# The order of VectorE's work in the attention head loop: logits and normalisations of a head pair side by side, then token shifts, evictions and selection rounds

## The chip, the cores and the metric

The kernel runs on one core of one Trainium2 chip. Its time is the device time of one launch in microseconds (us); shown are the median, the lowest and the highest of three runs, and one more execution was recorded by the hardware profiler. The engines are called by the profile's names: PE (TensorE, with PEld for its weight loads), DVE (VectorE), ACT (ScalarE), POOL (GpSimd) and SP (SyncE).

## The reference, cut to what matters

A step of a two-layer encoder over 512 prompt tokens and 64 sample tokens, `D_MODEL` 1024. Each layer projects the normalised input with one wide matrix (`w_in`); its columns go to three branches (RWKV-7 time mixing, sparse attention, retention) and to gates. The change lies in the sparse attention and in what runs beside it, the first steps of the RWKV branch:

```python
# sparse attention: an indexer scores keys, the best topk of them are kept for each query
score = einsum(relu(qi . ki), wi) * INDEX_SCALE          # masked to admissible keys
_, idx = lax.top_k(score, topk)                          # 128 of up to 512, 144 for the sample
logits = einsum(q, k_sel) * SA_HEAD_DIM ** -0.5
p = softmax(logits)
o = einsum(p, v_sel)                                     # 8 heads, 2 key/value heads
...
# RWKV: token shift of the projected columns P, 14 tiles of 128 columns
X = P + (prev - P) * rwkv_mu                             # prev: the row before, per token
```

## The kernel before, in words

All activations are kept transposed, 128 channels on the partitions and tokens (576 = 512 + 64) along the free axis. Projections run in float32 split into a high and a low part, so one slice of a dense tile (128 output columns, 128 of the 1024 inputs) is six matmuls of 288 columns, and a tile has `KT = 8` slices. Weights come by SP's queue, POOL splits them, and PE multiplies. Every engine executes a program of its own, in the order in which it is written out by hand, and waits on semaphores where it needs another.

The stage of the change is the **head loop** of each layer's sparse attention. There are 40 runs: run = 8 * b + h, with four blocks `b` of 128 queries (128, 256, 384 and 512 keys) and h = 0 to 7 heads, and then block 4, the 64 sample queries. Runs 0 to 31 are taken in 16 pairs (run, run + 1); even runs use half 0 and odd runs half 1 of the PSUM and SBUF buffers. A head goes through these steps:

- `scores` (PE, L559): query times keys into `mix[half]`. It first waits until the logits of run - 2 have left that buffer.
- `logits` (DVE, L1981 and L1984): scales, adds the mask of the selected keys, takes the row maximum and its negative.
- `exps` (ACT): the exponential and its row sum (an ACTIVATE and a READ_ACCUMULATOR).
- `normalised` (DVE, L2084 and L2086): reciprocal of the sum, then the multiplication of the probabilities.
- `turn_head` (PE, L984) transposes the probabilities, `turned_head` (ACT) copies them, `values` (PE) multiplies them by v, `out_head` (ACT) copies the result out. `turn_head(run)` waits for `normalised(run)` and for `out_head(run - 2)`.

Three other things are done beside the heads. PE **fills**: after `turn_head` of a pair it multiplies the next slices of the RWKV and gate projections, 10 slices a pair in blocks 0 to 2 and 8 in block 3 (`FILL_STEP`). A finished tile is evicted from PSUM by DVE: `shift_raws` (L2054 to L2061) multiplies it by the row norms into the two-buffered `pt`, or, for the tiles from 14 on, `gate_scaled` (L2040) does so into a gate buffer; both free the PSUM buffer. ACT's `filled` then multiplies `pt` by `mu` into the single buffer `d_t` (or, for a gate, starts the store to memory with `gate_away`), and DVE's `token_shift` (L2069) adds the other half and frees `d_t` with `shift_dve`. And DVE does the **selection rounds** of the next blocks (`rounds_beside`: `topk`, each round a MAX8 L1949 and a MATCH_REPLACE8 L1951, each behind a drain L1675); `STEP_ROUNDS` says which rounds belong to which run.

DVE's order in an iteration of the pair loop is: the rounds of run, `normalised` of both heads, `shift_raws` of the tiles that ended in the fill of the pair before (`arrived`), the rounds of run + 1, `token_shift` of the same tiles, `logits` of the next pair. ACT's order is `out_head` of the pair before, `turned_head` of this pair, `filled`, `exps` of the next pair. Counted from the two lists (`fill_range`, `done`), `arrived` holds one tile in most iterations, two at runs 8, 16 and 24 (tiles 4 and 5, 9 and 10, 14 and 15). At run 2, the rotary step of tile 15 (`rope`, L1715 to L1721) stands first.

Of the kernel before, what the change touches and what calls it, by code (L numbers as in the profile page):

```python
# [38 lines left out]
KT = D // P  # L39
# [20 lines left out]
N_RET, N_SA, N_RW, N_GATE = 16, 9, 14, 24  # L60
# [87 lines left out]
def fill_range(b, h):  # L148

    first = KT + 8 * sum(FILL_STEP[:b]) + h * FILL_STEP[b]  # L150
    return first, first + FILL_STEP[b]


def mid_range(step):
# [13 lines left out]
def done(first, end):  # L168

    return range(first // KT, end // KT)  # L170
# [55 lines left out]
def build(nc, dr, outs):  # L226
    with ExitStack() as ctx:
# [907 lines left out]
        def _(act):  # L1135
# [206 lines left out]
            with act.Fori(0, DEPTH) as l:  # L1342
# [65 lines left out]
                def exps(b, h):  # L1408
                    n, keys = (P, (b + 1) * P) if b < 4 else (C, T)
                    half, run = h % 2, b * 8 + h  # L1410
                    act.wait_ge(at_logits, l * 40 + (run + 1))
                    if run >= 2:

                        act.wait_ge(at_turned, l * 40 + (run - 1))
                    op(prob[0:n, half, 0:keys], logit[0:n, half, 0:keys], ACT.Exp,
                       bias=stat[0:n, half, 1:2], accum_out=stat[0:n, half, 2:3]).then_inc(at_exp, 1)

                piece = 0
                for t in range(3, N_SA):
# [14 lines left out]
                    if t >= 5:  # L1434
                        b = t - 4
# [17 lines left out]
                def filled(tiles):  # L1453

                    for f in tiles:
                        if f >= N_RW:
                            gate_away(l, f - N_RW, gate_dsa)
                            continue
                        act.wait_ge(shift_raw, l * N_RW + (f + 1))
                        if f >= 1:  # L1460
                            act.wait_ge(shift_dve, l * N_RW + f)
                        op(d_t, pt[:, f % 2, 0:TX], ACT.Copy, scale=pr("mu", f)).then_inc(shift_mu, 1)
# [57 lines left out]
                waiting = [0]  # L1520
                ended = [[], []]
                for run in range(0, 32, 2):
                    b, h = run // 8, run % 8
                    if run:
                        out_head(run - 2)
                        out_head(run - 1)
                    turned_head(run)
                    turned_head(run + 1)
                    filled(waiting)
                    waiting = list(done(fill_range(b, h)[0], fill_range(b, h + 1)[1]))  # L1530
                    if run < 30:
                        for r in (run + 2, run + 3):
                            exps(r // 8, r % 8)
                out_head(30)
                for run in range(31, 40):
                    b, h = run // 8, run % 8
# [133 lines left out]
        def _(dve):  # L1670
# [216 lines left out]
            with dve.Fori(0, DEPTH) as l:  # L1887
# [203 lines left out]
                    for rounds in STEP_ROUNDS.get(run, ()):  # L2091
                        topk(*rounds)

                arrived = [0]
                logits(0, 1)
                for run in range(0, 32, 2):
                    b, h = run // 8, run % 8
                    if run == 2:
                        rope(l, 15, s_raw, s_tcos, s_trot, s_cos, s_sin, ysa[:, 3, :])
                        settle()  # L2100

                    rounds_beside(run)
                    normalised(run)
                    normalised(run + 1)
                    shift_raws(arrived)
                    rounds_beside(run + 1)
                    token_shift(arrived)
                    arrived = list(done(fill_range(b, h)[0], fill_range(b, h + 1)[1]))
                    if run < 30:
                        for r in (run + 2, run + 3):  # L2110
                            logits(r // 8, r % 8)
                assert all(t >= N_RW for t in arrived)
                shift_raws(arrived)
                logits(4, 0)

                ended = []
# [269 lines left out]
```

## Time and profile before

| | |
|---|---|
| time, median of 3 runs | 2569.2 us |
| lowest and highest | 2565.81 and 2570.72 us |
| time of the profiled execution | 2568.46 us |
| its span, first to last instruction | 2566.7 us |
| busy PE, PEld, DVE, ACT, POOL | 2481.8, 2351.5, 1221.2, 588.8, 1344.2 us |
| mean granted TensorE clock | 0.982 |
| head loop of layer 0, pairs 0 to 30 | about 240 to 412 us of the span |
| the same of layer 1 | about 1510 to 1682 us |

The page gives the busy time of each engine over the whole span; the other views give groups of instructions, waits, the chain of work that ended last, and the instructions in order of time. A clock of 1.00 is 2.4 GHz, 0.50 is 1.2 GHz. Times of instructions are us from the start of the span.

### The profile page before, as it was taken

Reading aid. Unit: us, or ns where it says so; the run is one execution under the profiler, and the core shown is the slowest. Engines: PE = TensorE matmul, PEld = TensorE weight load, DVE = VectorE, ACT = ScalarE, POOL = GpSimd, SP = SyncE. Lnnn points to the kernel's source line nnn. Section 1 sums busy time; section 2 is a strip of 40 time slices with the busy share of each in tenths; the row PEclk is TensorE's granted clock in tenths of the full one; section 3 lists DMA queues with packets and bytes.
Section 4 is the critical chain, followed back from the end, with each engine's and each line's share of the span. In section 5 each row is a group of like instructions: output and inputs, shape, how many; then the busy total and the mean of one; then the engine's idle time right before and its main releaser. Section 6 shows DMA issues by size and latency. Waiting matters only on the chain.

```text
span 2566.7 us, 62432 instructions
## 1 busy us (share of the span) xinstructions
PE 2481.8 (97%) x24614; PEld 2351.5 (92%) x24614; DVE 1221.2 (48%) x2248; ACT 588.8 (23%) x1155; POOL 1344.2 (52%) x1780
## 2 busy tenths in 40 slices
PE   8998999999989999999999989999999899999998
PEld 7997888899979999999999978888999799999998
DVE  5357886544465322121443578856544653121224
ACT  4122233322232211011230223233221422010112
POOL 7634443512137766666775445434222477666665
PEclk9999999999999999999999999999999999999999
DMA  5212112311144222222242221223111442222221
GB/s 207 92 38 90 58 59 97 116 40 41 42 166 152 82 89 83 82 82 82 82 151 71 68 77 58 72 80 115 41 36 61 173 138 83 83 83 82 82 82 70
DMA packets 67690, 223.78 MB, mean 87 GB/s; under 512 B 8736, under 2 KB 9632, under 8 KB 66432
## 3 DMA queue, kind: packets, MB, share of 16 engines
q1 hardware_dynamic: 44496, 159.08, 18.5%
q10 hardware_dynamic: 22960, 61.34, 6.9%
q8 instruction: 177, 2.90, 0.5%
q14 instruction: 57, 0.47, 0.1%
HBM read 190.25 MB, written 29.03 MB: 85 GB/s over the span
## 4 chain that ended last, share of the span: by engine, by line
PE 85%; DVE 7%; DVEq 4%; issue 2%; ACT 1%; DMA 1%; ACTq 1%; POOL 0%; SPq 0%
PE dense L559 70%; PE mix L559 13%; DVEq L1675 3%; DVE region_b L1949 1%; DVE region_b L2069 1%; DVE region_b L1981 1%; PE mix L984 1%; POOL w_lo L546 0%; DVE region_b L2086 0%; DMA region_b<-region_b 0%; ACT in_hi L1137 0%; DVE x L1951 0%; DVE x L1967 0%; ACT region_b L1137 0%; DVE region_b L2055 0%
## 5 line engine op out<-in xcount | busy, mean ns | idle before, releaser
L542 POOL TENSOR_SCALAR w_hi<-w_raw 128x512 fp32r<-128x512 f32 x592 | 381.7, 663 | 1177.0 <-PE dense L559 928.9
L546 POOL TENSOR_TENSOR w_lo<-w_raw,w_hi 128x256 fp32r<-128x256 f32 x1184 | 962.5, 844 | 24.7
L559 PE MATMUL dense<-in_hi,w_hi 128*128 128x288 f32 x2432 | 680.0, 294 | 16.2 <-DVE in_lo L2181 15.3
L559 PE MATMUL dense<-act_hi,w_hi 128*128 128x288 f32 x2272 | 677.1, 309 | 17.5 <-POOL w_lo L546 12.6
L559 PE MATMUL dense<-in_lo,w_hi 128*128 128x288 f32 x2432 | 679.1, 295 | 0.0
L559 PE MATMUL dense<-act_lo,w_hi 128*128 128x288 f32 x2272 | 652.4, 298 | 0.0
L559 PE MATMUL dense<-act_hi,w_lo 128*128 128x288 f32 x2272 | 538.7, 298 | 0.0
L559 PE MATMUL dense<-in_hi,w_lo 128*128 128x288 f32 x2432 | 522.9, 297 | 0.0
L559 PEld LDWEIGHTS dense<-in_hi,w_hi 128*128 128x128 f32 x2432 | 459.1, 189 | 18.5 <-DVE in_lo L2181 16.8
L559 PEld LDWEIGHTS dense<-act_hi,w_hi 128*128 128x128 f32 x2272 | 436.1, 192 | 35.5 <-DVE act_lo L1693 11.1
L559 PEld LDWEIGHTS dense<-in_lo,w_hi 128*128 128x128 f32 x2432 | 459.4, 189 | 0.0
L559 PEld LDWEIGHTS dense<-act_lo,w_hi 128*128 128x128 f32 x2272 | 436.6, 192 | 0.0
L559 PEld LDWEIGHTS dense<-in_hi,w_lo 128*128 128x128 f32 x2432 | 390.8, 189 | 0.0
L559 PEld LDWEIGHTS dense<-act_hi,w_lo 128*128 128x128 f32 x2272 | 387.0, 191 | 0.0
L2248 DVE SCALAR_TENSOR_TENSOR y_mix<-dense,n_root 128x576 f32<-128x576 f32 x64 | 48.5, 758 | 296.6 <-PE dense L559 282.9
L1137 ACT ACTIVATE y_mix<-y_mix 128x576 f32<-128x576 f32 x64 | 44.0, 687 | 604.0 <-DVEq L2251 604.0
L1137 ACT ACTIVATE region_b<-region_b 128x576 f32<-128x576 f32 (+7 forms) x166 | 106.3, 642 | 312.8 <-DVE region_b L1984 115.5
L1137 ACT ACTIVATE region_b<-mix 128x256 f32<-128x256 f32 (+5 forms) x194 | 77.9, 419 | 344.7 <-PE mix L559 242.1
L2263 DVE TENSOR_TENSOR x<-x,dense 128x576 f32<-128x576 f32 x48 | 36.2, 755 | 252.6 <-PE dense L559 252.6
L559 PE MATMUL mix<-region_b 64*64 64x64 f32 (+5 forms) x2008 | 121.2, 240 | 2.5 <-ACT y_mix L1137 2.5
L559 PEld LDWEIGHTS mix<-region_b 64*64 64x64 f32 (+3 forms) x2008 | 101.5, 142 | 20.6 <-issue 19.3
L1137 ACT ACTIVATE region_b<-dense 128x256 f32<-128x256 f32 (+4 forms) x134 | 64.5, 494 | 191.0 <-PE dense L559 137.6
(201 smaller groups left out, 2513.8 us busy)
## 6 DMA issues: line engine op xcount, KB each, us to landing
w_raw<-in_stream SPq DMA_DIRECT2D x296, 512.0 KB, 3.3
region_b<-gate_scratch ACTq DMA_DIRECT2D x48, 288.0 KB, 2.9
gate_scratch<-region_b ACTq DMA_DIRECT2D x36, 288.0 KB, 2.2
x_scratch<-x ACTq DMA_DIRECT2D x2, 2304.0 KB, 13.2
y_scratch<-y_mix ACTq DMA_DIRECT2D x2, 2304.0 KB, 7.5
x<-x_scratch ACTq DMA_DIRECT2D x2, 2304.0 KB, 10.1
y_mix<-y_scratch ACTq DMA_DIRECT2D x2, 2304.0 KB, 9.0
gate_scratch<-region_a ACTq DMA_DIRECT2D x12, 288.0 KB, 2.4
```

Source lines behind the costliest of these rows:

```text
L542: hi = nc.gpsimd.tensor_scalar(w_hi[:, v, c], w_raw[:, s, c], 1.0, 1.0, ALU.mult, ALU.mult)
L546: lo = nc.gpsimd.tensor_tensor(w_lo[:, v, c], w_raw[:, s, c], w_hi[:, v, c].bitcast(F32), ALU.subtract)
L559: return nc.tensor.matmul(out, lhsT, rhs, start=start, stop=stop, skip_group_check=True)
L984: mm = nc.tensor.transpose(out[half][0:w, kb * n:(kb + 1) * n], prob[0:n, half, kb * P:kb * P + w], ident[0:n, 0:n])
L1137: return nc.scalar.activation(out, in_, func, **kw)
L1675: v.drain()
L1949: v.max(out=top8[0:n], in_=sc)
L1981: v.tensor_tensor_reduce(logit[0:n, half, 0:keys], mix[half][0:n, 0:keys], sa_bias[b][0:n, 0:keys], SA_SCALE, -3.0e38, ALU.add, ALU.max, s ...
L2069: v.scalar_tensor_tensor(shifted[t], pt[:, t % 2, 1:TX + 1], mu_own[:, t:t + 1], d_t, ALU.mult, ALU.add).then_inc(shift_dve, 1)
L2248: v.scalar_tensor_tensor(halves(relu_m[:, m % 2, :]), out_of(dense[m % 2]), 0.0, halves(n_rs), ALU.max, ALU.mult).then_inc(dense_free[m % ...
L2263: v.tensor_tensor(halves(x[:, m, :]), halves(x[:, m, :]), out_of(dense[m % 2]), ALU.add).then_inc(dense_free[m % 2], 1)
```

## The change

DVE's iteration becomes: `normalised` of both heads of the pair (right behind the `logits` that ended the iteration before), the rotary step at run 2, `token_shift` of the tiles that were evicted before, `shift_raws` of the late tiles of the pair before, the rounds of run and of run + 1 in one piece, `shift_raws` of the early tiles of this same pair, `logits` of the next pair. A new function `pair_done` names the tiles that end in a pair's fill and counts those that end in its first four slices as early. ACT does `filled` behind `exps` of the next pair, not ahead of it, for the late tiles of the pair before and the early ones of this pair. By the two lists, the early tiles are 3, 4, 8, 9, 13 and 14 (evicted at runs 4, 6, 12, 14, 20 and 22), all others are late, and `token_shift` has two tiles at runs 6, 14 and 22 (tiles 2 and 3, 7 and 8, 12 and 13). PE's program is not changed.

```diff
@@ -149,6 +149,14 @@
     first = KT + 8 * sum(FILL_STEP[:b]) + h * FILL_STEP[b]
     return first, first + FILL_STEP[b]
+def pair_done(run):
+    first, end = fill_range(run // 8, run % 8)[0], fill_range(run // 8, run % 8 + 1)[1]
+    tiles = list(done(first, end))
+    return tiles, sum(1 for t in tiles if (t + 1) * KT - first <= 4 and run < 30)
 def mid_range(step):
@@ -1526,11 +1534,12 @@
                         out_head(run - 1)
                     turned_head(run)
                     turned_head(run + 1)
-                    filled(waiting)
-                    waiting = list(done(fill_range(b, h)[0], fill_range(b, h + 1)[1]))
                     if run < 30:
                         for r in (run + 2, run + 3):
                             exps(r // 8, r % 8)
+                    tiles, early = pair_done(run)
+                    filled(waiting + tiles[:early])
+                    waiting = tiles[early:]
                 out_head(30)
                 for run in range(31, 40):
                     b, h = run // 8, run % 8
@@ -2091,26 +2100,28 @@
                     for rounds in STEP_ROUNDS.get(run, ()):
                         topk(*rounds)
-                arrived = [0]
+                shifting, late = [], [0]
                 logits(0, 1)
                 for run in range(0, 32, 2):
-                    b, h = run // 8, run % 8
+                    normalised(run)
+                    normalised(run + 1)
                     if run == 2:
                         rope(l, 15, s_raw, s_tcos, s_trot, s_cos, s_sin, ysa[:, 3, :])
                         settle()
+                    token_shift(shifting)
+                    shift_raws(late)
                     rounds_beside(run)
-                    normalised(run)
-                    normalised(run + 1)
-                    shift_raws(arrived)
                     rounds_beside(run + 1)
-                    token_shift(arrived)
-                    arrived = list(done(fill_range(b, h)[0], fill_range(b, h + 1)[1]))
+                    tiles, early = pair_done(run)
+                    shift_raws(tiles[:early])
+                    shifting, late = late + tiles[:early], tiles[early:]
                     if run < 30:
                         for r in (run + 2, run + 3):
                             logits(r // 8, r % 8)
-                assert all(t >= N_RW for t in arrived)
-                shift_raws(arrived)
+                assert all(t >= N_RW for t in shifting + late)
+                shift_raws(late)
                 logits(4, 0)
                 ended = []
```

## Rows read from the trace of the kernel before

**Rows 1.** Page: busy us (share of the span) and instructions, by engine

```profile
PE 2481.8 (97%) x24614; PEld 2351.5 (92%) x24614; DVE 1221.2 (48%) x2248; ACT 588.8 (23%) x1155; POOL 1344.2 (52%) x1780
```

**Rows 2.** Busy time by stage of layer 0: span, engines, clock, DMA

```profile
235.00:412.00 177.00, 166.05 (x1187) 150.69 (x1186) 148.93 (x424) 50.92 (x139) 78.05 (x111) 0.94 0.19 64
```

**Rows 3.** Waits of 225 to 415 us: engine, line, releaser, total, times, longest

```profile
PE mix L984 <- DVE region_b L2086: 9.5, 5, 3.0
...
DVE region_b L2069 <- ACT region_b L1137: 2.1, 3, 0.9
```

**Rows 4.** Timeline of PE, layer 0: transposes; start, us, [idle before]

```profile
255.78 0.88 PE L984 MATMUL mix<-cst,region_b 128*128 128x128 f32 x2 [2.88 <-DVE region_b L2086]
...
347.51 1.51 PE L984 MATMUL mix<-cst,region_b 128*128 128x128 f32 x6 [3.00 <-DVE region_b L2086]
...
382.88 1.09 PE L984 MATMUL mix<-cst,region_b 128*128 128x128 f32 x8
383.73 0.38 PE L559 MATMUL dense<-act_hi,w_hi 128*128 128x288 f32 x1
```

**Rows 5.** Timeline of PE, layer 1, the transpose of run 18

```profile
1617.28 1.51 PE L984 MATMUL mix<-cst,region_b 128*128 128x128 f32 x6 [3.00 <-DVE region_b L2086]
```

**Rows 6.** PE by stretch around run 18: busy, granted clock, DMA

```profile
347.50:352.50 5.00, 4.99 (x22) 0.50 0.03 11
```

**Rows 7.** Timeline of DVE at the loop's start

```profile
239.78 0.15 DVE L1984 TENSOR_SCALAR region_b<-region_b 128x1 f32<-128x1 f32 x1
...
242.24 0.16 DVE L2084 RECIPROCAL region_b<-region_b 128x1 f32<-128x1 f32 x1
...
242.91 0.15 DVE L2084 RECIPROCAL region_b<-region_b 128x1 f32<-128x1 f32 x1
```

**Rows 8.** Timeline of ACT at the loop's start

```profile
241.07 0.59 ACTq L1451 DMA_DIRECT2D out_ik_new<-region_b  x1
...
242.09 0.19 ACT L1137 ACTIVATION_READ_ACCUMULATOR region_b<-region_b 128x1 f32 x1
```

**Rows 9.** Timeline of DVE, normalisation, two-tile shift, logits' end

```profile
284.98 0.16 DVE L2084 RECIPROCAL region_b<-region_b 128x1 f32<-128x1 f32 x1
...
285.49 0.15 DVE L2084 RECIPROCAL region_b<-region_b 128x1 f32<-128x1 f32 x1
...
286.12 0.13 DVE L2054 COPY region_b<-par 128x1 f32<-128x1 f32 x1
...
291.73 0.82 DVE L2069 SCALAR_TENSOR_TENSOR region_b<-region_b,mu_own 128x577 f32<-128x577 f32 x1
293.46 0.82 DVE L2069 SCALAR_TENSOR_TENSOR region_b<-region_b,mu_own 128x577 f32<-128x577 f32 x1 [0.91 <-ACT region_b L1137]
...
365.77 0.16 DVE L1984 TENSOR_SCALAR region_b<-region_b 128x1 f32<-128x1 f32 x1
```

**Rows 10.** Timeline of ACT, mu product and exponentials

```profile
292.64 0.78 ACT L1137 ACTIVATE region_b<-region_b,par 128x577 f32<-128x577 f32 x1 [4.78 <-DVE region_b L2069]
...
296.54 0.19 ACT L1137 ACTIVATION_READ_ACCUMULATOR region_b<-region_b 128x1 f32 x1
296.63 0.55 ACT L1137 ACTIVATE y_mix<-mix 64x128 f32<-64x128 f32 x2
...
366.48 0.19 ACT L1137 ACTIVATION_READ_ACCUMULATOR region_b<-region_b 128x1 f32 x1
```

**Rows 11.** Timeline of DVE, rounds and normalisations of run 24, gates

```profile
378.71 0.74 DVE L1949 MAX8 region_b<-x 64x8 f32<-64x576 f32 x1
...
380.42 0.16 DVE L2084 RECIPROCAL region_b<-region_b 128x1 f32<-128x1 f32 x1
...
381.30 0.61 DVE L2086 TENSOR_SCALAR region_b<-region_b 128x512 f32<-128x512 f32 x1
381.83 1.40 DVE L2040 TENSOR_TENSOR region_a<-dense,n_root 128x576 f32<-128x576 f32 x2
```

**Rows 12.** Timeline of DVE behind the pair loop

```profile
421.72 0.76 DVE L2040 TENSOR_TENSOR region_a<-dense,n_root 128x576 f32<-128x576 f32 x1 [6.61 <-PE dense L559]
```

## Prediction

> **What bounds the kernel now.** The page comes first: PE is busy for 2481.8 of 2566.7 us, DVE for 48% of it [rows 1]. Over the span PE sets the time, and whatever DVE does is worth only what PE waits for it. The second view is therefore the busy time of the stage alone. In the head loop of layer 0 PE is busy for 166.05 of 177 us and DVE for 148.93, and the granted clock is 0.94 [rows 2]; the reader is to see that here DVE is no longer at half load. Third, the waits of that stretch: PE's transposes wait for the normalisation (L2086) five times, 9.5 us in total and 3.0 at the longest, while DVE waits for ACT's mu product three times, 2.1 us in all [rows 3]. The view names no wait of DVE for PE between the first pair and the end of the selection rounds. DVE's other free time lies between its own instructions, in drains. Fourth, the timeline of PE: the long waits are at run 2 (2.88 us) and run 18 (3.00 us) [rows 4], and layer 1 has 3.00 us at run 18 as well [rows 5]. Right behind the wait of run 18 PE runs for 5.00 us at a granted 0.50, the 1.2 GHz level [rows 6], so such a wait costs up to 2.5 us more.
>
> The point that I take from this: from the first pair on **DVE's own chain is the slow one** and PE keeps up with it. Behind run 18 PE no longer waits, but it is just in time: at run 24 the second normalisation ends at 381.30 + 0.61 = 381.91 and PE's transposes begin at 382.88, a slack of 0.97 us [rows 4, 11]. So DVE may be late by about one us there before PE is late, and a gain is limited likewise. Behind the loop there is room: DVE sits idle for 6.61 us before the last gate eviction [rows 12].
>
> **The change part by part.** No operation is added or removed; DVE's sum of work stays. What changes is what DVE has done by each normalisation, since this releases PE, and where DVE waits for ACT. I follow DVE to the normalisation of run 24, the first pair behind the last iterations with much work (20 and 22), where the slack is 0.97. All terms are per layer.
>
> *The rounds go behind the normalisation.* At run 24 one round of 576 keys no longer stands in front: from 378.71 to 380.42 [rows 11], **-1.71**. That is the gain of the change. At run 2 the rotary step goes behind too, so the wait of 2.88 should vanish; but DVE does that work afterwards and the next pairs get it.
>
> *A gate eviction goes ahead.* Tile 14 is early at run 22 and so comes before the normalisation of run 24. Two took 1.40 us [rows 11]: **+0.70**. The other tiles up to 13 are evicted and shifted before that point in either order.
>
> *The start.* Before, the rounds of run 0 hid ACT's lateness. The logits of run 1 end at 239.78 + 0.15 = 239.93, the second reciprocal came 0.67 us behind the first [rows 7], and so DVE would get to it at about 240.6 if the first starts at once. But ACT issues transfers (the last begins at 241.07, 0.59 us) and the sum of exponentials of run 1 is read only at 242.09 + 0.19 = 242.28 [rows 8]. With no rounds in between DVE sits idle for 242.3 - 240.6 = **+1.7**. PE gains 0.6 there, which does not help the chain.
>
> *The normalisations wait for the exponentials.* At run 22 the second logits end at 365.77 + 0.16 = 365.93 and the second sum is read at 366.48 + 0.19 = 366.67 [rows 9, 10], 0.74 us later. In an unbroken normalisation pair the second reciprocal comes 284.98 to 285.49 = 0.51 behind the first [rows 9], so some 0.58 behind the logits. The wait is up to 0.16; with fewer keys the exponential is shorter. For 12 pairs (runs 2 to 24) the bounds are 0 and 1.9; I take 0.12 each, since the row of run 22 is a long one: **+1.4**.
>
> *The token shift waits for the mu product.* `filled` now stands behind the exponentials. ACT starts an instruction 0.09 behind the start of such a read (296.54, 296.63), so the product, 0.78 us long [rows 10], ends about 0.74 - 0.10 + 0.78 = 1.42 behind the logits. DVE gets to the shift after the pair of normalisations, 286.12 - 284.98 = 1.14 [rows 9], and is there 1.2 to 1.37 behind the logits. Before, a set of rounds hid the product. Ten pairs (4 to 22), bounds 0 and 2.1, I take 0.13 each: **+1.3**.
>
> *Two tiles at once.* The second product needs `d_t` free and so waits for the first shift: 291.73, product at 292.64, second shift at 293.46 after 0.91 us idle [rows 9, 10]. This exists before and after; now it comes at three iterations (6, 14, 22), and all waits of this kind took 2.1 before [rows 3]: 3 x 0.91 - 2.1 = **+0.6**.
>
> Sum: -1.71 + 0.70 + 1.7 + 1.4 + 1.3 + 0.6 = **+4.0** on DVE's chain at run 24; by the low bounds +1.3, by the high ones +5.3. PE's share is 4.0 - 0.97 = 3.0. The reader should also follow ACT: in the two-tile iterations its second `filled` waits for a shift of the next iteration, and `out_head` and with it PE's transposes stand behind it, some 2 us longer than the normalisation alone would keep them. At run 22 this is covered by the wait at run 24 that follows; without that cover it is up to 2 us more. The gate stores start later on ACT's queue, but two iterations pass before their buffer is wanted again: nothing.
>
> Last, the clock. DVE's heavy iterations (late and early evictions at 20, two shifts at 22) now follow each other, so I expect PE to wait for about 3 us at run 24, as at run 18 before. Whether the clock falls there and costs 2.5 us [rows 6] is open; bounds 0 and 2.5 in each layer. PE has only the slack of its last pairs to win it back. I take it in one of two layers. Total: 2 x 3.0 + 2.5 = **+8.5 us** on the profiled execution's 2568.46 us (span 2566.7 and 1.8 around it): **2577.0 us**. That execution lies 0.7 under the median of the runs shown, 2569.2. About 0.2%, 5.1 us, is what a measurement of this kernel can tell from no change.
>
> **The rivals.**
>
> *A: the waits of DVE for ACT are hidden.* If the normalisation and shift terms are near 0, DVE is late by 1.3 and PE by 0.3: 2569.1 us; with half of those terms, PE is 1.7 late without a fall of the clock: 2571.9. For it: the exponential of the first head is done before the second logits are, and each wait that I charge is under 0.2 us. Against it: the start alone costs what the rounds give. This is no measurable change.
>
> *B: faster, because PE is what sets the loop.* Then its waits go away: 9.5 us per layer [rows 3]. The mechanism: each pair's probabilities are ready one set of rounds earlier, and a wait of 3.0 would fall to 1.3 by the 1.71 us of a single round, and further where two rounds stood in front. It decides if DVE has time to spare, so that the work put behind the normalisations is done while PE fills. With all waits gone 2568.5 - 19 = 2549.5; with a third, 2562. The Trainium skill, Perfetto Trace Analysis, Identifying the Most-Contended Engine, would take the engine with the highest occupancy as the bottleneck, and for TensorE weight loads, not matmuls; in this stage that is 150.69 us of weight loads against 148.93 of DVE, so by that rule PE stays in front and the time is B's. Against B: DVE's rest is no waiting for PE, and from run 24 on the slack is under one us.
>
> *C: slower by more.* All waits at their high bounds, 5.3 - 0.97 = 4.3, the clock falls in both layers: 2 x (4.3 + 2.5) = 13.6, 2582; with `out_head` behind the product 2 us more in each layer, 2586. For it: every one of these chains goes through ACT's single queue.
>
> **How the numbers follow.** Forecast (2574.5 without a fall of the clock to 2579.5 with two): 0.48. A: 0.27. B: 0.11. C: 0.14. Faster is B, 0.11; the same is A, 0.27; slower is the forecast and C, 0.62. For 8 in 10 the range leaves out most of B and the end of C: 2565 to 2586.
>
> **What would show it.** Right, if the profile of the changed kernel has DVE idle for 1.5 to 2 us before a reciprocal at the start of each loop with ACT as the releaser; small waits of reciprocals and shifts for ACT in nearly every pair; three waits of 0.9 at shifts; PE without a wait at run 2 and with long ones at runs 8, 16 and 24; and the transposes of run 30 some 3 to 5 us later from the loop's start than before. Wrong, if PE has no wait behind run 10, or if those last transposes come no later: then DVE's chain was not the limit or its waits were covered.

## The result, and the profile of the changed kernel

The changed kernel takes 2581.73 us (median of six runs, 2577.95 to 2584.06) beside 2568.97 (six runs, 2565.57 to 2572.3): a ratio of 1.005, 95% interval 1.0038 to 1.0061. It is slower. The profiled execution takes 2581.09 us with a span of 2579.3, against 2568.46 and 2566.7: +12.6, where +8.5 was forecast.

The head of the page answers to [rows 1]:

```profile
PE 2489.6 (97%) x24614; PEld 2355.3 (91%) x24614; DVE 1225.4 (48%) x2248; ACT 585.8 (23%) x1155; POOL 1342.4 (52%) x1780
```

The counts of instructions are the same, so no work was added; DVE's sum has grown by 4.2 us all the same, to which the last parts come back. Next, the waits of 225 to 425 us in layer 0 (engine, line, releaser: total, times, longest), which answer to [rows 3]. PE's transposes are now L992, its other products L567, the reciprocals L2093, the multiplications L2095, the token shift L2078, the first instruction of an eviction L2063, the end of the logits L1993.

```profile
PE mix L992 <- issue: 5.5, 3, 2.3
...
PE mix L567 <- DVE region_b L1993: 4.4, 6, 1.8
...
DVE region_b L2093 <- ACT region_b L1145: 3.6, 9, 1.9
...
DVE region_b L2063 <- issue: 2.9, 13, 0.2
PE mix L992 <- ACT y_mix L1145: 2.8, 4, 0.9
DVE region_b L2078 <- ACT region_b L1145: 2.7, 3, 0.9
...
PE mix L992 <- DVE region_b L2095: 1.1, 2, 0.7
```

PE's waits for normalisations have gone from 9.5 us to 1.1. In their place stand three waits put down to "issue" (that is, to nothing the view can name), waits of the score products for logits, and waits for ACT's copies. DVE's own idle time is of several kinds, shown one by one below.

The first stands at the start of the loop; DVE's timeline there (start, duration, instruction, idle before it and its releaser) answers to [rows 7]:

```profile
236.71 0.15 DVE L2093 RECIPROCAL region_b<-region_b 128x1 f32<-128x1 f32 x1
236.94 0.29 DVE L2095 TENSOR_SCALAR region_b<-region_b 128x128 f32<-128x128 f32 x1
239.18 0.16 DVE L2093 RECIPROCAL region_b<-region_b 128x1 f32<-128x1 f32 x1 [1.94 <-ACT region_b L1145]
```

The second is one of the three two-tile iterations, on DVE, ACT and PE in turn:

```profile
272.67 0.82 DVE L2078 SCALAR_TENSOR_TENSOR region_b<-region_b,mu_own 128x577 f32<-128x577 f32 x1
274.39 0.82 DVE L2078 SCALAR_TENSOR_TENSOR region_b<-region_b,mu_own 128x577 f32<-128x577 f32 x1 [0.90 <-ACT region_b L1145]
```

```profile
271.88 0.76 ACT L1145 ACTIVATE region_b<-region_b,par 128x577 f32<-128x577 f32 x1
273.58 0.78 ACT L1145 ACTIVATE region_b<-region_b,par 128x577 f32<-128x577 f32 x1 [0.95 <-DVE region_b L2078]
274.27 0.55 ACT L1145 ACTIVATE y_mix<-mix 64x128 f32<-64x128 f32 x2
```

```profile
274.62 0.30 PE L992 MATMUL mix<-cst,region_b 128*128 128x128 f32 x1 [2.16 <-issue]
...
323.55 0.45 PE L992 MATMUL mix<-cst,region_b 128*128 128x128 f32 x1 [2.26 <-issue]
...
373.74 0.30 PE L992 MATMUL mix<-cst,region_b 128*128 128x128 f32 x1 [1.10 <-issue]
```

Read across: the second mu product on ACT sits 0.95 us for DVE's first shift; `out_head`'s copies to `y_mix` stand behind it in ACT's queue, and PE's transposes go as soon as the first copy is done. So the "issue" waits of PE at runs 6, 14 and 22 are the hold behind the second `filled`; I call them the holds. Behind the first two the clock falls in this layer, behind the third it does not; PE's stretches that begin at these transposes (length; PE busy; granted clock; DMA) answer to [rows 6]:

```profile
274.60:279.60 5.00, 4.98 (x25) 0.66 0.01 2
323.50:328.50 5.00, 4.95 (x21) 0.50 0.01 3
373.70:378.70 5.00, 4.96 (x38) 1.00 0.00 0
```

Third, one iteration with a single shift:

```profile
284.82 0.16 DVE L2093 RECIPROCAL region_b<-region_b 128x1 f32<-128x1 f32 x1 [0.17 <-ACT region_b L1145]
285.06 0.57 DVE L2095 TENSOR_SCALAR region_b<-region_b 128x256 f32<-128x256 f32 x1
285.56 1.16 DVE L2078 SCALAR_TENSOR_TENSOR region_b<-region_b,mu_own 128x577 f32<-128x577 f32 x1
286.95 0.15 DVE L2063 COPY region_b<-par 128x1 f32<-128x1 f32 x1 [0.24 <-issue]
```

A small wait for the exponentials (0.17), no wait for the mu product, and a gap of 0.24 before the eviction, where an eviction directly behind a normalisation began 0.08 before that one's end [rows 11].

At run 24 the fill starts without a wait, DVE's two reciprocals, then PE; this answers to [rows 4, 11]:

```profile
384.52 0.15 DVE L2093 RECIPROCAL region_b<-region_b 128x1 f32<-128x1 f32 x1
...
385.49 0.16 DVE L2093 RECIPROCAL region_b<-region_b 128x1 f32<-128x1 f32 x1 [0.24 <-ACT region_b L1145]
```

```profile
385.78 1.22 PE L992 MATMUL mix<-cst,region_b 128*128 128x128 f32 x8
386.75 0.38 PE L567 MATMUL dense<-act_hi,w_hi 128*128 128x288 f32 x1
```

These times cannot be set against those of before directly, since the loops begin at different places. I count from a `memset` of DVE at the loop's head (239.05 and 1509.12 us before, 235.91 and 1515.61 after), which I call the origin. Three marks are used from here on: the first reciprocal of run 24 (384.52 - 235.91 = 148.61 after, 380.42 - 239.05 = 141.37 before), the loop's length (up to the logits of the tail head that follows the pair loop), and PE's dense work at run 24 (386.75 - 235.91 = 150.84 against 383.73 - 239.05 = 144.68). In the changed kernel DVE reaches run 24 later by 7.24 us (6.69 in layer 1), PE fills later by 6.16, and the loop is longer by 6.34 us in layer 0 and 6.60 in layer 1. The two sum to 12.9, against 12.6 in the span. The three stretches outside the loops (ahead of the first, between them, behind the second) differ by -3.1, +3.3 and -0.5 us, which sum to -0.3: on balance the whole loss lies in the two head loops.

### The profile page after: what moved, and what is told of

Same layout as the page of the kernel before. It is cut to its first block, busy times and chain, and to the rows that moved or that the text cites. A ratio compares the mean times of both kernels' runs of the same rounds, so it can differ in the third digit from the quotient of the medians.

```text
span 2579.3 us, 62432 instructions
## 1 busy us (share of the span) xinstructions
PE 2489.6 (97%) x24614; PEld 2355.3 (91%) x24614; DVE 1225.4 (48%) x2248; ACT 585.8 (23%) x1155; POOL 1342.4 (52%) x1780
## 4 chain that ended last, share of the span: by engine, by line
PE 83%; DVE 7%; DVEq 4%; issue 3%; ACT 2%; ACTq 1%; DMA 1%; POOL 0%; SPq 0%
PE dense L567 69%; PE mix L567 13%; DVEq L1684 3%; DVE region_b L1958 2%; ACT region_b L1145 1%; DVE region_b L1990 1%; DVE region_b L2078 1%; PE mix L992 0%; POOL w_lo L554 0%; ACT in_hi L1145 0%; DMA region_b<-region_b 0%; DVE region_b L2065 0%; DVE x L1960 0%; ACTq L1218 0%; ACTq L1219 0%
## 5 line engine op out<-in xcount | busy, mean ns | idle before, releaser
L550 POOL TENSOR_SCALAR w_hi<-w_raw 128x512 fp32r<-128x512 f32 x592 | 374.9, 651 | 1191.5 <-PE dense L567 951.5
L567 PE MATMUL dense<-in_hi,w_hi 128*128 128x288 f32 x2432 | 680.1, 294 | 15.2 <-DVE in_lo L2192 14.6
L567 PE MATMUL dense<-act_hi,w_hi 128*128 128x288 f32 x2272 | 678.5, 309 | 15.7 <-POOL w_lo L554 12.1
L567 PE MATMUL dense<-in_lo,w_hi 128*128 128x288 f32 x2432 | 679.1, 295 | 0.0
L567 PE MATMUL dense<-act_lo,w_hi 128*128 128x288 f32 x2272 | 653.5, 299 | 0.0
L567 PE MATMUL dense<-act_hi,w_lo 128*128 128x288 f32 x2272 | 539.3, 299 | 0.0
L567 PE MATMUL dense<-in_hi,w_lo 128*128 128x288 f32 x2432 | 523.0, 296 | 0.0
L567 PEld LDWEIGHTS dense<-in_hi,w_hi 128*128 128x128 f32 x2432 | 459.4, 189 | 18.0 <-DVE in_lo L2192 16.1
L567 PEld LDWEIGHTS dense<-act_hi,w_hi 128*128 128x128 f32 x2272 | 436.5, 192 | 32.8 <-DVE act_lo L1702 11.0
L567 PEld LDWEIGHTS dense<-in_lo,w_hi 128*128 128x128 f32 x2432 | 459.7, 189 | 0.0
L567 PEld LDWEIGHTS dense<-act_lo,w_hi 128*128 128x128 f32 x2272 | 437.0, 192 | 0.0
L567 PEld LDWEIGHTS dense<-in_hi,w_lo 128*128 128x128 f32 x2432 | 391.1, 189 | 0.0
L567 PEld LDWEIGHTS dense<-act_hi,w_lo 128*128 128x128 f32 x2272 | 387.5, 192 | 0.0
L567 PE MATMUL mix<-region_b 64*64 64x64 f32 (+5 forms) x2008 | 121.0, 240 | 2.5 <-ACT y_mix L1145 2.5
L567 PEld LDWEIGHTS mix<-region_b 64*64 64x64 f32 (+3 forms) x2008 | 101.3, 142 | 20.7 <-issue 19.4
```

The lines of the kernel that those rows point to most:

```text
L550: hi = nc.gpsimd.tensor_scalar(w_hi[:, v, c], w_raw[:, s, c], 1.0, 1.0, ALU.mult, ALU.mult)
L567: return nc.tensor.matmul(out, lhsT, rhs, start=start, stop=stop, skip_group_check=True)
```

## The experiments

All times are medians; "before" is the kernel before, run beside it. The ratio and its interval are taken over the single runs, so the ratio is not quite the quotient of the two medians. "Run 24" and "loop" are the marks above, for layers 0 / 1, from one profiled execution of each kernel. The two layers run the same loop and their marks differ by up to 1.6 us, so a difference well under that is not to be trusted.

| kernel | us | before, us | ratio (95%) | run 24 | loop |
|---|---|---|---|---|---|
| before | 2568.97 | | | 141.37 / 141.62 | 183.83 / 183.25 |
| changed | 2581.73 | 2568.97 | 1.005 (1.0038-1.0061) | 148.61 / 148.31 | 190.17 / 189.85 |
| e1_start | 2578.26 | 2568.35 | 1.0041 (1.0026-1.0055) | 146.01 / 146.29 | 189.33 / 188.19 |
| e2_act | 2578.28 | 2568.35 | 1.0041 (1.0026-1.0055) | 147.12 / 146.63 | 189.07 / 188.60 |
| e3_evict_first | 2579.49 | 2568.35 | 1.0034 (1.0019-1.0048) | 145.73 / 144.92 | 187.74 / 186.70 |
| e4_norm_only | 2583.84 | 2568.35 | 1.0068 (1.0051-1.0085) | 147.51 / 146.86 | 192.45 / 191.89 |
| e5_two_mu | 2577.77 | 2566.43 | 1.0036 (1.0019-1.0052) | 146.40 / 145.93 | 188.41 / 187.65 |
| e6_all_three | 2560.19 | 2566.43 | 0.998 (0.996-0.9999) | 142.08 / 141.52 | 183.80 / 183.60 |
| e7_before_two_mu | 2560.59 | 2566.43 | 0.9971 (0.9954-0.9988) | 139.25 / 139.15 | 182.50 / 180.93 |
| e8_norm_evict | 2569.73 | 2566.43 | 1.0006 (0.999-1.0022) | 142.49 / 143.87 | 185.43 / 186.92 |
| e9_before_fewer | 2563.41 | 2569.54 | 0.9973 (0.9959-0.9986) | 136.62 / 137.09 | 179.50 / 180.10 |
| e9_after_fewer | 2566.93 | 2569.54 | 0.9991 (0.9982-1.0001) | 141.70 / 141.00 | 183.26 / 182.53 |

The theory: DVE's chain sets the head loop, and the change adds idle time and slower instructions to that chain. The rivals: ACT's hold of `out_head` is what costs, through PE's waits and clock; or PE sets the loop and DVE's lateness is covered.

**e1_start.** One cost is taken away: run 0's rounds go back ahead of the first normalisation.

```
                 for run in range(0, 32, 2):
+                    if run == 0:
+                        rounds_beside(run)
                     normalised(run)
                     normalised(run + 1)
...
-                    rounds_beside(run)
+                    if run:
+                        rounds_beside(run)
                     rounds_beside(run + 1)
```

> The changed kernel, but the rounds of run 0 stand ahead of the first normalisations again. Theory 1 (VectorE's own chain up to the normalisation of run 24 sets the loop, and its idle wait of 1.94 us for ScalarE's first exponential is part of what was added): the chain is 1.8 us shorter per layer and TensorE follows in full, 3.5 us below the changed kernel, about 9 us above the kernel before. Theory 2 (ScalarE's queue, with the copies of the results behind the mu products, sets TensorE): the wait at the start is not what counts, no more than 1 us of change. Theory 3 (the clock): no change, 12 to 13 us above.

DVE's chain at run 24 shortens by 2.60 / 2.02 us, but the loop only by 0.84 / 1.66. PE's transposes at run 22 show why:

```profile
374.70 1.51 PE L992 MATMUL mix<-cst,region_b 128*128 128x128 f32 x6 [2.15 <-issue]
```

With DVE earlier, the hold at run 22 is 2.15 us where it was 1.10, and behind it the granted clock over 5 us is 0.50 where it was 1.00, so in layer 0 part of the gain goes into the next limit. In layer 1 the hold was 2.15 already and the clock behind it is 1.00 where it was 0.66; there the loop follows by most of the gain. The start wait is real and costs what was forecast or a little more; the hold, with the clock behind it, is a second limit close behind.

**e2_act.** ACT's order: the waiting tile's product goes ahead of the exponentials, only the early tile's stays behind them.

```
                     turned_head(run + 1)
+                    filled(waiting)
                     if run < 30:
...
-                    filled(waiting + tiles[:early])
+                    filled(tiles[:early])
```

> The changed kernel, but ScalarE makes the mu product of the late tiles ahead of the exponentials of the next pair, as before the change; only the early tiles' products stay behind them. Theory 1: the shift of a single tile does not wait for ScalarE in the changed kernel's trace, so VectorE's chain stays, within 1 us of the changed kernel. Theory 2: the copies of the results come 0.8 us sooner in most pairs and TensorE's transposes with them, 4 to 8 us below the changed kernel.

Run 24 is earlier by 1.49 / 1.68 and the loop shorter by 1.10 / 1.25, more than the first theory had and far from the second. The three holds stay (2.00, 2.09 and 2.06 us at runs 6, 14 and 22), so this order of ACT does not make them.

The expectation had one thing wrong: single shifts do wait for the product, by less than the 0.15 us that the views name. In the changed kernel seven of the ten shifts behind a normalisation in layer 0, and eight in layer 1, start 0.03 to 0.04 us behind the end of ACT's product. Run 4, ACT and DVE in the changed kernel:

```profile
260.69 0.76 ACT L1145 ACTIVATE region_b<-region_b,par 128x577 f32<-128x577 f32 x1
```

```profile
261.06 0.29 DVE L2095 TENSOR_SCALAR region_b<-region_b 128x128 f32<-128x128 f32 x1
261.48 0.82 DVE L2078 SCALAR_TENSOR_TENSOR region_b<-region_b,mu_own 128x577 f32<-128x577 f32 x1
```

The product ends at 261.45, 0.10 behind the normalisation's end. With the product done early the same shift starts 0.09 ahead of that end:

```profile
259.42 0.29 DVE L2096 TENSOR_SCALAR region_b<-region_b 128x128 f32<-128x128 f32 x1
259.62 0.81 DVE L2079 SCALAR_TENSOR_TENSOR region_b<-region_b,mu_own 128x577 f32<-128x577 f32 x1
```

Over the ten shifts this run takes 0.80 / 1.07 us of such idle time away.

**e3_evict_first.** On DVE the late eviction goes ahead of the shift, so that it follows a normalisation again.

```
-                    token_shift(shifting)
                     shift_raws(late)
+                    token_shift(shifting)
```

> The changed kernel, but the evictions of the late tiles come ahead of the token shifts, right behind the normalisations. Theory 1: of what VectorE's chain has gained in length some 0.24 us per iteration is the gap ahead of an eviction that follows a shift and its drain; behind a normalisation there was none before. Nine evictions of that kind: 2.1 us less per layer, 4 us below the changed kernel. If the gap moves to the shift instead, or the evictions now wait for TensorE: 0 to 1 us. Theory 2: no change.

By the marks this is the largest single effect: 2.88 / 3.39 at run 24 and 2.43 / 3.15 in the loop. The timed runs do not rank e1, e2, e3 and e5 (ratios 1.0034 to 1.0041), and the profiled execution of e3 was no shorter than that of the changed kernel, as the stretches outside its loops took 6.3 us more. The waits of DVE name where it comes from:

```profile
DVE region_b L2063 <- issue: 1.0, 5, 0.2
```

The gap ahead of an eviction is gone in eight of its 13 places, 1.9 us of named idle time. The rest is less exactly placed: evictions and shifts also ran shorter, 0.82 and 0.34 us in layer 0, and normalisations 0.72 longer (sums of all their rows).

**e4_norm_only.** From the other side: the kernel before, with only its normalisations moved ahead of the rotary step and of the rounds of `run`; evictions and shifts stay behind them.

```
                     b, h = run // 8, run % 8
+                    normalised(run)
+                    normalised(run + 1)
                     if run == 2:
...
                     rounds_beside(run)
-                    normalised(run)
-                    normalised(run + 1)
                     shift_raws(arrived)
```

> The kernel before, but the normalisations of a pair stand ahead of the rounds of run; evictions, shifts, early and late tiles and ScalarE's order are those before the change. Theory 1: VectorE's chain at run 24 has +1.8 from the start, +2 from the exponentials and -1.7 from the round that goes behind, 2.1 us; less 1 us of slack that is 1.1 us per layer: 2 us above the kernel before, 10 below the changed kernel, so most of the loss is from the other half of the change. Theory 2: ScalarE's queue is that of before, so none of the loss is left: at the kernel before or up to 5 us below it, as the probabilities come earlier.

It is the slowest of all, 192.45 / 191.89, and some 15 us above the kernel before, where one theory had 2 above and the other none. Of its waits of PE over the whole program the longest in sum is this:

```profile
PE dense L559 <- DVEq L2060: 20.1, 14, 3.4
```

Before, this wait (PE's dense work for an accumulator in PSUM that DVE has yet to evict) was 1.4 us in four. In DVE's list the evictions stand behind the same work as before; but the fill now starts a set of rounds sooner, and so asks for its accumulators sooner than they are free. DVE's chain is also late by 6.14 / 5.24 at run 24, with waits for the exponentials (3.9 us in ten in layer 0, six of them up to run 24) and gaps ahead of the evictions (2.2 in ten); this run does not part the two. What follows: an earlier normalisation alone moves PE's wait from the transposes to the accumulators, so moving the evictions too was a necessary part of this change.

**e5_two_mu.** The changed kernel with a second mu buffer, in space that is free during the loop, so that the second product need not wait for the first shift.

```
+        d_two = [d_t, region_b[:, cw.at - 2 * T:cw.at - 2 * T + TX]]
...
-                        if f >= 1:
-                            act.wait_ge(shift_dve, l * N_RW + f)
-                        op(d_t, pt[:, f % 2, 0:TX], ACT.Copy, scale=pr("mu", f)).then_inc(shift_mu, 1)
+                        if f >= 2:
+                            act.wait_ge(shift_dve, l * N_RW + f - 1)
+                        op(d_two[f % 2], pt[:, f % 2, 0:TX], ACT.Copy, scale=pr("mu", f)).then_inc(shift_mu, 1)
...
-                        v.scalar_tensor_tensor(shifted[t], pt[:, t % 2, 1:TX + 1], mu_own[:, t:t + 1], d_t, ALU.mult,
+                        v.scalar_tensor_tensor(shifted[t], pt[:, t % 2, 1:TX + 1], mu_own[:, t:t + 1], d_two[t % 2], ALU.mult,
...
```

> The changed kernel with a second buffer for the mu product (tiles in turn), so that ScalarE's second product no longer waits for VectorE's first shift, and the copies of the results behind it are not held. Theory 1 (VectorE's chain): three waits of 0.90 us go, the chain at run 24 is 2.7 us shorter per layer. Theory 2 (the hold in ScalarE's queue at runs 6, 14 and 22, seen as waits of 2.2 us of TensorE's transposes): the transposes of these runs come 2 us sooner as well, and the clock does not fall behind them. Both together: 5 to 8 us below the changed kernel, 5 to 8 above the kernel before; if neither is on the path: no change.

Run 24 is earlier by 2.21 / 2.38, the loop shorter by 1.76 / 2.20; the time is 4 us under the changed kernel, less than the 5 to 8 expected. DVE's wait for the product (2.7 us in three) is gone from the waits, and PE's holds are now these:

```profile
PE mix L993 <- issue: 3.4, 3, 1.2
```

The holds fell by 2.1 us, so the single buffer makes that part of them; what keeps PE for the other 1.1 to 1.2 us each was not looked into. DVE's chain fell by 2.2, so this run alone does not tell the chain from ACT's hold as the cause. e3 does: it leaves the "issue" waits nearly as they were (4.9 us in three, before it 5.5), with the waits for ACT's copies even longer (4.6 us, before it 2.8), and still shortens the loop by more than e5.

**e6_all_three.** e1, e3 and e5 together, in the changed kernel.

> The changed kernel with all three: the rounds of run 0 ahead, the late evictions ahead of the shifts, two buffers for the mu product. Theory 1: the chain at run 24 falls by 2.4 + 3.1 (as measured singly) + 2.7 = 8.2 us from 148.5, to 140 us behind the loop's start, 1 us ahead of the kernel before, and nothing holds TensorE at runs 6, 14 and 22: 0 to 3 us below the kernel before. If TensorE's own work or another hold sets the loop by now, only half of that comes: 4 to 7 us above the kernel before.

The loop is 183.80 / 183.60 us, that of the kernel before (183.83 / 183.25). The single effects on run 24 sum to 7.69 / 7.79 and together give 6.53 / 6.79. So taking the three away wins back as much as was lost. Not all of that was the loss, though: the second buffer also takes away waits that the old order has (e7). Against e7, with that buffer on both sides, the new order's loops are still longer by 1.30 / 2.67 us and its run 24 later by 2.83 / 2.37; in the timed runs the two cannot be told apart (2560.19 and 2560.59). With the three costs gone the new order is worth nothing against the old one.

**e7_before_two_mu.** The second mu buffer of e5, in the kernel before.

> The kernel before with only the second buffer for the mu product. Theory 1: its two waits of 0.91 us per layer and the small one go from a chain that bounds the loop; TensorE has 1 us of slack there, so it gains what its own work lets it: 1 to 2 us per layer, 2 to 4 us below the kernel before. If TensorE's work behind run 18 sets the end: the wait of 3.0 us at run 18 falls by 1.8, 3 to 4 us in all; if neither: no change.

The simplest version that beats both: 2560.59 us, 0.1 to 0.5% under the kernel before, with one buffer more and the old order. Run 24 is earlier by 2.12 / 2.47 and the loops are shorter by 1.33 / 2.32. The two shifts that were 291.73 and 293.46, with 0.91 us between them [rows 9], now run on:

```profile
291.56 1.74 DVE L2070 SCALAR_TENSOR_TENSOR region_b<-region_b,mu_own 128x577 f32<-128x577 f32 x2
293.65 0.43 DVE L1982 CUSTOM_DVE_ANT_0 region_b<-mix,x 128x256 f32<-128x256 f32 x1 [0.35 <-issue]
```

Taking some 2 us of waiting out of DVE's chain shortens the loop by two thirds to nearly all of it: in the kernel before, too, DVE's chain carries the loop.

**e8_norm_evict.** The kernel before with two mu buffers and, from run 2 on, normalisations, then evictions, ahead of the rounds; the shifts stay behind the rounds, where their products are covered.

```
+                    if run == 0:
+                        rounds_beside(run)
+                    normalised(run)
+                    normalised(run + 1)
                     if run == 2:
...
-                    rounds_beside(run)
-                    normalised(run)
-                    normalised(run + 1)
                     shift_raws(arrived)
+                    if run:
+                        rounds_beside(run)
                     rounds_beside(run + 1)
                     token_shift(arrived)
```

> The kernel before with the normalisations ahead of the rounds (but not at run 0), the evictions of the pair before right behind them, then all rounds, then the shifts; ScalarE's queue as before the change, two buffers for the mu product; no early tiles. Theory 1: at run 24 -1.7 for the round that goes behind, -2.1 for the waits for mu, +1.5 to 2 for the waits for the exponentials: 2 us less chain than before; 2 to 6 us below the kernel before. Theory 2 (TensorE's work and holds): the waits at runs 2, 10 and 18 go, 5 to 10 us below.

No measurable change against the kernel before, where both theories had it faster, and slower than e7 by 9 us, with loops longer by 2.93 / 5.99. Of PE's waits over the whole program this one is new:

```profile
PE mix L560 <- DVE region_b L1985: 12.1, 12, 2.2
```

At the transposes PE waits for normalisations for 3.9 us, where e7 has 23.3. What it no longer waits for there it waits for at the scores, because the logits come later by the rounds that were moved. Normalising early with its costs removed brings nothing.

**e9_before_fewer and e9_after_fewer.** Both kernels without the selection rounds of runs 2 to 5, 9.6 us of DVE's time in each layer.

```
                     for rounds in STEP_ROUNDS.get(run, ()):
-                        topk(*rounds)
+                        if not 2 <= run <= 5:
+                            topk(*rounds)
```

> The kernel before without the selection rounds of runs 2 to 5 (eight rounds, 9.6 us of VectorE in each layer; the selection is then not the reference's). Theory 1 (VectorE's chain sets the loop's length): the normalisation of run 24 comes 9.6 us sooner and the loop is shorter by as much as TensorE's own work allows; the waits at runs 10 and 18 (5.8 us) and the falls of the clock behind them (up to 5 us) go: 6 to 9 us per layer, 12 to 18 us below the kernel before. If TensorE sets it: at most 2 us below.

> The changed kernel without the same rounds. Theory 1: the chain falls by 9.6 us from 148.5 us to 139 us at run 24 and the loop with it, 8 to 9.6 us per layer: 4 to 7 us below the kernel before, still some 10 us above the kernel before without the same rounds. Theory 2 (holds in ScalarE's queue): the holds at runs 6, 14 and 22 stay, with three falls of the clock: 0 to 4 us above the kernel before. If TensorE's own work sets it: no change, 12 us above.

The changed kernel's loop gives 6.91 / 7.32 of the 9.6 us back, that of the kernel before only 4.33 / 3.15. In the latter DVE's shifts then wait for ACT's product for 6.3 us in layer 0, where it was 2.1 [rows 3], and one of these waits is new and long:

```profile
DVE region_b L2069 <- ACT region_b L1137: 6.3, 4, 4.1
```

It stands at run 4, where rounds were taken out that had covered it: the product comes behind `out_head`'s copy, and that copy waits 4.08 us for PE's product with v. In the changed kernel DVE meets a limit too, 2.69 us before the early eviction of run 4:

```profile
264.23 0.15 DVE L2063 COPY region_b<-par 128x1 f32<-128x1 f32 x1 [2.69 <-PE dense L567]
```

So at the place where the rounds went, DVE's chain is longer than that of PE and ACT by only some 3 to 4 us a layer in the kernel before, and by some 7 in the changed one; rounds of other runs were not tried. I had expected 6 to 9 in the kernel before and 8 to 9.6 in the changed one, which came out some 2.6 us under the kernel before, not clear of noise, and not 4 to 7: the two chains lie closer together than my theory had it.

## Why the prediction was right, and where its sum was wrong

The sign, the place and the range are right: slower, through DVE's chain in the two head loops, 2581.7 within 2565 to 2586. The forecast of +8.5 us was 4.1 short, and its sum holds errors of opposite sign.

**What bounds the kernel.** Right. e6, e7 and e9 show that the loop's length follows DVE's chain. The slack of PE at run 24 is as read in layer 0: the chain is late by 7.24 and PE's dense work by 6.16, so 1.08 was absorbed, forecast 0.97. The forecast took the same for layer 1, and there it does not hold: before the change the second normalisation ended at 1652.22 and PE's transposes began at 1652.34, a slack of 0.12, and 0.22 was absorbed (6.69 on the chain, 6.47 on PE's dense work).

**DVE's chain at run 24.** This is the step that failed in size: +4.0 forecast, +7.24 / +6.69 measured. Layer 0, term by term:

- Rounds behind: one round less stands in front, as forecast (DVE's 576-key scans up to that point are 6 where they were 7), -1.57 by its instructions' durations against -1.71 from start to start.
- Gate ahead: forecast +0.70, measured 0.76 by its duration.
- Start: forecast +1.7, measured 1.94 of idle time (1.87 more than between two other such instructions), and e1 gives 2.60 / 2.02 back.
- Normalisations: forecast +1.4. Eight waits for the exponentials are named, 3.6 - 1.94 = 1.7 us, six of them up to run 24. By all rows the idle time inside the pairs grows by 4.42, of which 1.87 is the start, so 2.5; but the normalisations themselves run 1.66 us shorter in sum, so the net is 0.9.
- Shifts of single tiles: forecast +1.3, measured 1.0. No such wait is named, but most of the ten shifts behind normalisations start as the product ends. On average they start 0.01 us behind the normalisation's end (0.03 in layer 1), where those that find the product done start 0.08 ahead of it; e2 gives 0.80 / 1.07 back.
- Two tiles: forecast +0.6, measured 3 x 0.90 - 1.82 = 0.88.

These give some 3.8, near the 4.0 forecast, so the terms of the sum were about right in total. The other 3.4 us stood in no term, and that is where the sum failed. They come from all rows of DVE's timeline between the origin and run 24, durations and the idle time between them summed for each kind. Instructions that stand in front of run 24 in both kernels run longer, by 2.9 us in sum: selection rounds 1.1, the rotary step 0.9, shifts 0.6, evictions 0.4, logits -0.1. Idle time within the groups (other than normalisations and pairs of shifts) grows by 1.1. Between the groups it grows by 0.4, and without the waits of the shifts it shrinks by 0.6. Of the gaps between groups, eight of 0.23 between shift and eviction, five of 0.22 between rounds and an early eviction and six of 0.33 between rounds and logits come in; twelve of 0.35 between shift and logits go out, with smaller ones. In layer 1 the rotary step and the rounds run longer by about as much, the evictions by 0.7, the shifts not. My error was to price a moved instruction at its old duration and its old distance to its neighbour.

**The clock.** Forecast a fall behind a long wait at run 24 worth 2.5 us in one of two layers. PE had no wait there and its fill ran at full clock. The clock fell at other places: over 5 us it is 0.66 behind run 6 and 0.50 behind run 14, where the kernel before has 0.50 behind each of its long waits at runs 2, 10 and 18; in layer 1 it is 0.66 to 0.70 behind all three holds, before 0.50 behind runs 10 and 18. Over 184 us from the origin the mean granted clock is 0.95 against 0.94, in layer 1 0.96 in both. The term was worth nothing: 6.16 + 6.47 + 0 = 12.6, as in the span. So 2.5 us too much for the clock made up for part of the 6.6 us too little on PE's side; that the total came as near as it did is luck to that extent.

**Of the rivals.** A fell: the waits were not hidden; the start, the normalisations and the shifts together cost 3.8 us in layer 0. B fell: PE's waits for normalisations did vanish as that rival had it, 9.5 to 1.1 us, but they came back under other names. By the occupancy rule of the Trainium skill (Perfetto Trace Analysis, Identifying the Most-Contended Engine), which stood beside it, PE would have stayed in front; the runs disagree, since 9.6 us less of DVE's work shortened the changed loop by 7 while PE's work was the same. C had one part right: `out_head` is held behind the second product at runs 6, 14 and 22. It was charged as an end of the range; e1 shows that it is a limit only just behind DVE's chain, and so costs little by itself and takes back part of what is gained on that chain.

**What would show it.** Seen: the wait at the start; small waits of the reciprocals; three waits of 0.9 at shifts; no wait at run 2. Only in part: waits at single shifts, which are there but too short for the view to name. Missed: PE's long waits (runs 6, 14 and 22, not 8, 16 and 24). The transposes of run 30 come 6.2 us later from the origin (414.76 - 235.91 against 411.67 - 239.05), where I had said 3 to 5.

**What stays open.** Why the instructions run longer in their new places is not shown by an experiment. POOL's work beside them is the likeliest cause (below). Nor is it settled why the origin itself lies up to 5 us apart between executions of these kernels, 234.28 to 239.64 in layer 0. No mark above rests on it, as all are counted from the origin; a time of the whole program does, and so the marks are the finer measure.

## What to carry to other kernels

When the engine that sets the end works through a fixed list, putting one result ahead in the list only moves the wait to the next consumer; it pays if it removes idle time on that engine, and here it added some. Ask of every block that goes behind another what it was covering there (here rounds hid the exponentials and the mu product), and look first for the wait that exists in either order: with the old order, the second mu buffer alone gave as much as the best of the new orders did with it. Look below the shortest wait that a view names: ten waits of 0.1 us were worth 1.0 here. And give a moved instruction a range for its duration, from its own shortest and longest rows.

## What was not expected of the hardware

**The same shift takes 0.82 us or up to 1.38, and only beside POOL is it long.** Of the 56 token shifts of 128x577 in the two profiled executions, before and after, the 37 with no POOL instruction at the same time took 0.81 to 0.82, every one. Of the other 19, five took 0.82 and 14 took 1.10 to 1.38. The shift at 285.56 above took 1.16, beside these two groups of POOL:

```profile
284.87 1.23 POOL L550 TENSOR_SCALAR w_hi<-w_raw 128x512 fp32r<-128x512 f32 x2 [2.36 <-PE dense L567]
286.19 2.51 POOL L554 TENSOR_TENSOR w_lo<-w_raw,w_hi 128x256 fp32r<-128x256 f32 x3
```

The rotary step, three instructions of 0.75 us before, took 0.75, 1.28 and 1.14 after, all three beside POOL; two of those before were beside POOL too and took 0.75 and 0.76. The Trainium skill (SBUF — State Buffer, Who interferes with whom) says that a VectorE instruction with two inputs in SBUF contends with a GpSimd instruction that reads SBUF, and that issue order decides which of the two is kept out. The rows agree that only shifts beside POOL are long. On the order they are divided: of the five short ones three start before POOL's instruction and two 0.46 and 0.50 us behind it, and three of the long ones start 0.03 before it. No run here took POOL's work away, so this is a reading of rows and not an experiment.

**A gap whose size depends on what stands in front.** An eviction starts 0.24 us after the end of a shift (0.16 at the first), 0.22 after the end of a round, and 0.08 before the end of a normalisation. e3 changes only which of them the late evictions and the shifts follow, and the gap goes. In the kernel a shift and a round each end with a drain and the multiplication of a normalisation does not; whether that makes the gap was not tried.
